# Second block's output tiles apart in PSUM, the gate as three rounded products with its embedding between tiles, the down projection's rests all on VectorE

## What is computed

```python
# first block
x = x + rms_norm(mix, g_post_mix)                        # stick-breaking and latent attention
h = rms_norm(x, g_pre_ffn)
u = causal_depthwise_conv(h @ w_up, conv_w, conv_b)
gate, val = jnp.split(u, 2, axis=-1)
f = (jax.nn.gelu(gate, approximate=True) * val) @ w_down # the down projection, 2816 -> 1024
x = x + rms_norm(f, g_post_ffn)
e = p @ w_ple                                            # the embedding, 256 -> 1024
g = jax.nn.sigmoid(rms_norm(x, g_ple_gate) @ w_ple_gate + b_ple_gate)   # the gate, 1024 -> 1024
x = x + rms_norm(g * e, g_post_ple)
# second block, all its norms scaled and shifted by mod = silu(c) @ mod_w + mod_b
mix = jnp.concatenate([y_conv, y_att, y_pool], axis=-1) @ w_out         # 1024 -> 1024
x = x + g1 * mix
h = _rmsnorm(x, norm2_g) * (1 + sc2) + sh2
x = x + g2 * _hier_moe(h, ...)     # 32 experts of width 512; each token takes 2 of one group of 8
return _rmsnorm(x, final_g)
```

## Time and profile before

| | us |
|---|---|
| median of 3 runs | 1012.39 (1012.35 to 1013.99) |
| the profiled execution, its own time | 1006.37 |
| its span | 1004.7 |
| TensorE busy | 818.2 (81%) |
| VectorE, ScalarE, POOL busy | 320.2, 300.8, 134.6 |
| share of TensorE in the chain that ended last | 53% |
| share of transfers in it | 33% |

### The profile page before, as it was taken

The page is one execution under the profiler, slowest core; times in us unless marked ns, Lnnn a source line. Parts: engine busy times, 40 slices in busy tenths (PEclk is TensorE's granted clock), DMA queues, the critical chain, the costliest instruction groups (busy, mean ns, idle before and its releaser), DMA issues.

```text
span 1004.7 us, 12218 instructions
## 1 busy us (share of the span) xinstructions
PE 818.2 (81%) x5112; PEld 518.7 (52%) x5112; DVE 320.2 (32%) x682; ACT 300.8 (30%) x606; POOL 134.6 (13%) x146
## 2 busy tenths in 40 slices
PE   6998879999998999999978899676667665566755
PEld 5856346999997874487866634312222121122213
DVE  3306555666775441349651311001000000100001
ACT  2316355666664543545442211000100000000002
POOL 0011013344443100026400000000000000000000
PEclk9999989999999999999999999879988798897879
DMA  9932964445543555562717599999999999999995
GB/s 357 428 104 87 401 256 168 167 169 187 200 159 136 189 185 234 199 242 84 264 72 317 205 423 405 430 427 428 426 428 428 427 427 429 431 427 427 427 427 234
DMA packets 23678, 297.94 MB, mean 297 GB/s; under 512 B 2752, under 2 KB 3008, under 8 KB 5440
## 3 DMA queue, kind: packets, MB, share of 16 engines
q1 hardware_dynamic: 23616, 297.09, 73.0%
HBM read 296.03 MB, written 1.05 MB: 296 GB/s over the span
## 4 chain that ended last, share of the span: by engine, by line
PE 53%; DMA 33%; DVE 6%; ACT 5%; POOL 2%; issue 1%; SPq 0%; DVEq 0%; POOLq 0%
PE ps L186 53%; DMA ring<-in_exps 32%; ACT ar L200 1%; POOL ar L217 1%; DVE ar L206 1%; ACT yT L200 1%; DVE fr L206 1%; ACT ar L197 1%; DMA ring<-in_win 1%; ACT fr L197 0%; ACT sq L200 0%; DVE yT L214 0%; DVE misc L596 0%; DVE yT L206 0%; PE ps L619 0%
## 5 line engine op out<-in xcount | busy, mean ns | idle before, releaser
L186 PE MATMUL ps<-ring,sq 128*32 128x512 f32 x976 | 146.4, 739 | 72.6 <-DMA ring<-in_exps 72.1
L186 PE MATMUL ps<-ring,ar 128*32 128x512 f32 (+3 forms) x792 | 103.9, 612 | 48.0 <-DMA ring<-in_exps 40.8
L186 PE MATMUL ps<-fr 128*128 128x256 f32 (+1 forms) x756 | 122.5, 316 | 4.7 <-DVE fr L206 4.2
L186 PEld LDWEIGHTS ps<-ring,sq 128*32 128x32 f32 x976 | 30.6, 123 | 176.9 <-DMA ring<-in_exps 119.4
L186 PEld LDWEIGHTS ps<-fr 128*128 128x128 f32 x756 | 107.1, 191 | 15.7 <-DVE fr L206 3.8
L186 PE MATMUL ps<-hT,ring 128*128 128x256 f32 (+2 forms) x416 | 93.7, 386 | 7.1 <-DMA ring<-in_win 7.1
L186 PEld LDWEIGHTS ps<-hT,ring 128*128 128x128 f32 (+2 forms) x416 | 78.3, 190 | 21.1 <-DMA ring<-in_win 7.0
L206 DVE TENSOR_TENSOR ar<-ar,ps 128x512 f32<-128x512 f32 x9 | 6.2, 686 | 257.5 <-PE ps L186 257.5
L186 PEld LDWEIGHTS ps<-ring,ar 128*32 128x32 f32 (+1 forms) x792 | 27.2, 118 | 108.8 <-DMA ring<-in_exps 63.5
L186 PE MATMUL ps<-ar 128*128 128x512 f32 (+9 forms) x320 | 65.4, 435 | 16.3 <-DVE ar L206 8.9
L206 DVE TENSOR_TENSOR fr<-ring,fr 128x512 fp32r<-128x512 f32 x75 | 62.8, 855 | 44.3 <-ACT fr L197 44.0
(11 more groups left out here) (193 smaller groups left out, 944.8 us busy)
## 6 DMA issues: line engine op xcount, KB each, us to landing
ring<-in_exps SPq DMA_DIRECT2D x90, 2048.0 KB, 30.8
ring<-in_modw SPq DMA_DIRECT2D x12, 2048.0 KB, 8.3
ring<-in_wup SPq DMA_DIRECT2D x11, 2048.0 KB, 9.0
ring<-in_win SPq DMA_DIRECT2D x5, 2048.0 KB, 11.2
ring<-in_wdown SPq DMA_DIRECT2D x5, 2048.0 KB, 8.0
ar<-in_exps SPq DMA_DIRECT2D x3, 2048.0 KB, 12.8
ring<-in_wo SPq DMA_DIRECT2D x2, 2048.0 KB, 10.1
ring<-in_wgate SPq DMA_DIRECT2D x2, 2048.0 KB, 8.6
```

The costliest lines, as they stand in the source:

```text
L186: return pe(lambda e: e.matmul(o, l, r, start=start, stop=stop, skip_group_check=True), *waits, inc=inc)
```

## The change

It has five parts.

1. *Down projection.* All rests are made by VectorE; every fourth f had one on POOL. The pieces of the last two f for n=1 are made ahead of the matmuls and squares for n=0.
2. *Gate.* Its two operands are split, and 32 fp32 products become 96 rounded ones (`gate_parts`, `gate_low`, `gate`). The rests of the weights go to POOL, but for four that go to VectorE; the rests of the activations go to VectorE, each behind the addition of the next tile; the embedding's other three quarters stand between the tiles. Both gate slots are loaded ahead of a slot of `modw` and are given free when they are split.
3. *Output tiles of the second block.* `place` puts tiles 4 to 7 in banks 6, 2, 7 and 3, each alone; tiles 0 to 3 stay in pairs in banks 4 and 5, but both of a pair are computed before either is read. Logits and sums of tiles 2 and 3 come behind tiles 4 and 5.
4. *`over_tokens`* is split in four: two parts stand behind `token_major`, two before expert slots 2 and 3; it stood behind group 1. The third pair of `first_gather` uses bank 1 for both its tiles, and the second pair uses banks 2 and 3.
5. *Slot 6* of the experts no longer waits for the router (its biases moved to `cols`), and is issued ahead of slots 10 and 11.

```diff
         def down_parts(f, n):
-            return weight_parts(w_d[f // 4].ap((f % 4) * 1024 + 512 * n, 512), p_tt if f % 4 == 3 and n else v_tt, w_d[f // 4].ready)
+            return weight_parts(w_d[f // 4].ap((f % 4) * 1024 + 512 * n, 512), v_tt, w_d[f // 4].ready)
...
+        wps = [[down_parts(f, n) for f in (20, 21)] for n in range(2)]
         for n in range(2):
-            wps = [down_parts(f, n) for f in (20, 21)]
             for j in range(2):
-                for f, (i, wh, wl, t_w) in zip((20, 21), wps):
+                for f, (i, wh, wl, t_w) in zip((20, 21), wps[n]):
...
+        GX, GW = (4096, 6144), [8192 + 1024 * k for k in range(6)] + [WP, WP + 1024]
+        w_g = [stream("wgate", n) for n in range(2)]
+        g_free, wg = {}, {}
+
+        def gate_parts(n, k):
+            h, l = fr[:, GW[k]:GW[k] + 512], fr[:, GW[k] + 512:GW[k] + 1024]
+            wg[n, k] = h, l, split(w_g[n].ap(512 * k, 512), h, l, p_tt if n == 0 or k % 2 else v_tt, w_g[n].ready, t_down, g_free.get(k))
+
...
-        t_x = add_turned(TB, lambda k: col("g_post_ffn", k), tt)
-        th = [a_fn(tile(hT, k), tile(xT, k), ACT.Copy, t_x[k], t_down, scale=col("g_ple_gate", k)) for k in range(8)]
-        embed(1, 0)
-        embed(0, 1)
-        w_p.free(embed(1, 1))
+        for k in range(4):
+            gate_parts(0, k)
+        t_x, th = [], []
+
+        def gate_low(k):
+            hi, lo = (tile(fr, k, o) for o in GX)
+            t = a_fn(hi, tile(xT, k), ACT.Copy, t_x[k], t_down, scale=col("g_ple_gate", k))
+            th.append(v_stt(lo, tile(xT, k), col("g_ple_gate", k), hi.bitcast(F32), ALU.mult, ALU.subtract, t))
+
+        for k in range(8):
...
+            if k:
+                gate_low(k - 1)
+            if k == 3:
+                embed(1, 0)
+            elif k == 5:
+                embed(0, 1)
+            elif k == 7:
+                w_p.free(embed(1, 1))
+        gate_low(7)
+        for k in range(4, 8):
+            gate_parts(0, k)
+        w_g[0].free([wg[0, k][2] for k in range(4, 8)])
...
+        def gate(j, n, k):
...
+            mm(o, xh, wh, k == 0, False, t_w, th[k], read[ZB[j, n]])
+            mm(o, xl, wh, False, False)
+            t_gz[j, n] = g_free[k] = mm(o, xh, wl, False, k == 7, inc=1)
...
             for j in range(2):
-                o = k * S + 128 * j
-                t_gz[j, 0] = mm(bank(ZB[j, 0]), hT[:, o:o + 128], w.ap(k * 512, 512), k == 0, k == 7, w.ready, th[k],
-                               read[ZB[j, 0]], inc=int(k == 7))
+                gate(j, 0, k)
+            gate_parts(1, k)
...
-        rbias = ar[:, rbo:rbo + 36]
+        rbias = col("router_b", 0, 36)
...
+        place = {k: (4 + k // 2, S * (k % 2)) for k in range(4)}
+        place.update({4: (6, 0), 5: (2, 0), 6: (7, 0), 7: (3, 0)})
...
+        for i in range(2):
+            t = [wout2_tile(2 * i + n, (2, 3, 4, 5)) for n in range(2)]
+            for n in range(2):
+                residual(2 * i + n, t[1])
...
+        for k in range(4, 8):
+            t = wout2_tile(k, (0, 1, 6, 7, 2, 3, 4, 5))
+            if k < 6:
+                tile_logits(k - 2)
+                tile_squares(k - 2)
+            residual(k, t)
+            if k == 6:
+                for p in (4, 5):
+                    tile_logits(p)
+                    tile_squares(p)
...
+        def over_tokens(i):
+            for c in range(4):
+                k = 4 * (i % 2) + c
+                mm(bank(YB[i], 128 * c, 128 * c + 128), xT[:, k * S + 128 * (i // 2):k * S + 128 * (i // 2) + 128], ident,
+                   c == 0, False, tt[k], read[YB[i]])
+
+        for i in (2, 3):
+            over_tokens(i)
...
-        more = {3: ("more3", [hT[:, :], ar[:, 1536:3584]], t_early), 6: ("more6", spare, [t_arena, t_lg, read[LG]])}
+        more = {3: ("more3", [hT[:, :], ar[:, 1536:3584]], t_early), 6: ("more6", spare, t_arena)}
...
-                b, c = 2 + 2 * (p % 3) + k % 2, 0
+                b, c = (1, 128 * (k % 2)) if p == 2 else (2 + k % 2, 0)
...
-        placed = {j: stream("exps", j, extra=more.get(j)) for j in (0, 1, 2, 4, 3, 5, 7, 8, 9, 10, 11, 6)}
+        placed = {j: stream("exps", j, extra=more.get(j)) for j in (0, 1, 2, 4, 3, 5, 7, 8, 9, 6, 10, 11)}
...
+                    if j in (2, 3):
+                        over_tokens(j - 2)
...
-            if g == 1:
-                over_tokens()
```

More of the change, by code:

```diff
@@ L969, in build @@
                 r3, t_r3 = row_root(3, 32 * 1024, 120, t, S)
-        w.free(t_gz[1, 0])
-        w = stream("wgate", 1)
+        w_g[1].free([wg[1, k][2] for k in range(8)])
         for j in range(2):
             for k in range(8):
-                o = k * S + 128 * j
-                t = mm(bank(ZB[j, 1]), hT[:, o:o + 128], w.ap(k * 512, 512), k == 0, k == 7, w.ready, read[ZB[j, 1]], inc=int(k == 7))
-            t_gz[j, 1] = t
-        w.free(t)
+                gate(j, 1, k)
         for n in range(2):
@@ L1305, in wout2_tile @@
         def wout2_tile(k, ks):
-            i, n = k // 2, k % 2
-            b = 4 + i
+            b, o = place[k]
             for kk_ in ks:
-                t = mm(bank(b, n * S, n * S + S), w_2[i // 2].ap(kk_ * 512 + 256 * (i % 2) + 128 * n, 128), tile(yT, kk_),
-                       b not in started, kk_ == ks[-1], w_2[i // 2].ready, mixed[kk_], read[b], inc=int(kk_ == ks[-1]))
+                t = mm(bank(b, o, o + S), w_2[k // 4].ap(kk_ * 512 + 256 * (k // 2 % 2) + 128 * (k % 2), 128), tile(yT, kk_),
+                       b not in started, kk_ == ks[-1], w_2[k // 4].ready, mixed[kk_], read[b], inc=int(kk_ == ks[-1]))
@@ L1311, in wout2_tile, with residual @@
                 started.add(b)
+            return t
+        def residual(k, t):
+            b, o = place[k]
             x = tile(xT, k)
-            tt.append(v_stt(x, bank(b, n * S, n * S + S), mod[:, 16 + k:17 + k], x, ALU.mult, ALU.add, t, t_mod))
-            read[b] = tt[-1]
-            t_sq[k] = a_fn(tile(sq, k), x, ACT.Square, tt[-1], t_rc)
-            return t
-        for k in range(8):
-            t = wout2_tile(k, (2, 3, 4, 5) if k < 4 else (0, 1, 6, 7, 2, 3, 4, 5))
-            if k == 3 or k == 7:
-                w_2[k // 4].free(t)
-            for p in {3: (0, 1), 5: (2, 3), 6: (4, 5)}.get(k, ()):
-                tile_logits(p)
-                tile_squares(p)
+            read[b] = t = v_stt(x, bank(b, o, o + S), mod[:, 16 + k:17 + k], x, ALU.mult, ALU.add, t, t_mod)
+            tt.append(t)
+            t_sq[k] = a_fn(tile(sq, k % 4), x, ACT.Square, t, t_rc, t_sums.get(k - 4))
@@ new lines, in build @@
+        for i in range(2):
+            t = [wout2_tile(2 * i + n, (2, 3, 4, 5)) for n in range(2)]
+            for n in range(2):
+                residual(2 * i + n, t[1])
+            if i:
+                w_2[0].free(t[1])
+            if i:
+                for p in range(2):
+                    tile_logits(p)
[8 more added lines that the diff above has]
+                for p in (4, 5):
+                    tile_logits(p)
+                    tile_squares(p)
@@ L1325, in build @@
+        w_2[1].free(t)
         tile_logits(6)
```

31 lines of the change are left out of this document (18 added, 13 removed).

## The result

| | before | after |
|---|---|---|
| median of 4 runs, us | 1012.37 (1011.33 to 1013.99) | 995.85 (994.03 to 998.01) |
| the profiled execution, its own time | 1006.37 | 995.91 |
| its span | 1004.7 | 994.1 |

The ratio is 0.985, with an interval from 0.9818 to 0.9882. The forecast for the traced execution was 995.5 us and a span of 993.8; it came out at 995.91 and 994.1. (How far single executions of the kernel before differ, and what of the 16.5 us is chance, is the subject of the first experiment.)

A forecast was written before the change was run, and what follows sets the result against it. The end was taken to follow TensorE's use of slot 12; gains of 1.3 + 4.0 + 5.9 + 2.4 = 13.6 less 2.7 gave 10.9 us, so 995.5 for the traced execution and 1001.5 against the median, range 997.5 to 1005.5.

The forecast's parts named there:

- slot 0 at full clock: Rival, chance 0.15: expert slot 0 runs at 2.4 GHz and takes 1.7 us less; 12.6 in all, 999.8.
- Third f: Down projection: the last rest, moved from POOL to VectorE, is done 1.2 to 1.8 us earlier; 1.3 taken.
- Last two f: Down projection: pieces made ahead remove 2.27 us of idle time and 1.74 of half clock, 4.0 us.
- Gate: Gate product: 96 rounded products at 21.8 us replace fp32 ones at 27.8; gain 5.9 us after the switch.
- Tiles: Second block's output tiles: three odd tiles no longer wait for VectorE's read, 0.8 us each, 2.4 gained.
- x products: Token sums (over_tokens): eight products between slots 1 and 3 lose 1.9 us; eight before the rank's matmul are hidden.
- gathers: First gather, third pair: sharing bank 1, the second half waits for VectorE's read; 0.8 us lost, lower bound 0.5.
- Between 12 and 19: Expert slots: TensorE's way from slot 12's issue to slot 19's grows by 2.7 us, from 35.6 to 38.3.
- the end hangs on slot 19: Expert stream: slot 19 waits for TensorE's use of slot 12; behind it 77 slots at 4.91 us set the end.
- POOL did not starve the gate: Rival, chance 0.04: POOL's rests come too late for the gate's matmuls, making the kernel slower, 1014.4 and up.
- The stream followed: Rival, expert stream does not follow: 998.8 if the 2.7 us are all hidden, 1012.4 if something else holds it.
- Lost cover: Rival, chance 0.13: a late square, rest or clock fall in a denser stretch gives back 2 to 7 us, 1003.5 to 1008.5.

The follow-up runs named there:

- the first experiment: The kernel before, run again without an edit: ratio 1.0004 (0.9972 to 1.0035), 12 executions from 1005.76 to 1015.65 us.
- x_late: The changed kernel with the eight x products that stood before expert slots 2 and 3 put behind group 1: 994.43 us, ratio 0.9853.
- x_late_banks: The changed kernel with those eight x products behind group 1 and the third gather pair in banks 4 and 5: 994.94 us, ratio 0.9849.
- after_again: The changed kernel run once more, without a further edit: 996.09 us, ratio 0.9875, 6 executions from 995.07 to 999.63 us.
- best: x_late_banks plus 13 products of constants, which nobody reads, in TensorE's idle stretches at 73 to 77 us and 175 us: 991.30 us, ratio 0.9802.
- down_only: The kernel before with only the down projection's edits (all rests on VectorE, last two f's pieces made ahead): 1004.63 us, ratio 0.9948.

## Why the prediction was too careful

**The step that failed** is the last of the sum: "The median of the runs shown is 1012.39, 6.0 above the profiled one, so I set the difference against it: 1001.5." The sum itself was made for the traced execution, and there it gives 995.5 where 995.91 was measured. That it comes so close is in part luck: slot 19 went out at 597.93, 1.5 us earlier than the 599.4 forecast, and the stream behind it took 1.9 us longer than before in this one execution. I then carried the 6.0 us over as if they were a fixed addition that the changed kernel pays too. They were not: they are the distance between a lower and an upper execution of a kernel whose times have two heaps. The heaps' means are 7.1 us apart. After, there are no such heaps in 10 executions, and trace and median agree (995.91 and 995.85). Half of the executions of before lie in the upper heap; that all four first runs did was chance.

Against the mean of 108 executions the forecast difference of 10.9 would have given 999.8, inside the range and still 3.3 above the mean of after, 996.5. The rival below, with its 12.6, gives 998.1. The 1.6 us that are then left are over twice the standard error of the mean gain with all chips pooled (0.65), but on the one chip on which both kernels ran side by side nothing is left: the gain there is 12.5.

**The rival that came true**, in part beside the forecast: *slot 0 at full clock*. I gave it 0.15 because the matmuls ahead of slot 0 stay thin. Slot 0 is at full clock in both traces of the changed kernel; in the first it brought 1.56 us of the 1.7 forecast. With it the sum for slot 19 is 12.6; 12.37 was measured.

**The terms.** Third f 1.1 for 1.3: VectorE's rest begins when its own queue allows it, and TensorE is still idle for 1.30 us. Last two f 4.0 for 4.0. Gate 5.64 for 5.9. Tiles 2.5 for 2.4. x products -2.1 for -1.9, by a single edit; gathers -0.8 for -0.8, by an edit that also gives ScalarE its part back. Between 12 and 19 2.89 for 2.7. No term is off by more than 0.3 us.

**The structure.** That the end hangs on slot 19 held in the changed kernel: three kernels that issue it at different times (596.08 `x_late`, 600.83 `x_late_banks`, 597.93 after) end 378 to 380 us later. No matmul of the gate waits for a transfer.

**The other rivals.** POOL did not starve the gate: no row of it waits for POOL. The stream followed. *Lost cover* by a new fall of the clock happens in the changed kernel too: `after_again` has the clock at 0.75 over 76.6 to 83.4 us, the first trace of after at 0.50 from 495.0 to 505.2. The latter gave nothing back: the matmuls ahead of it and behind it lie 11.38 us earlier than before alike (487.97 against 499.35, 501.33 against 512.71). These rows answer to that:

```profile
76.60:83.40 6.80, 6.16 (x38) 4.80 (x39) 5.12 (x6) 5.39 (x8) 0.00 (x0) 0.75 0.60 255
```

```profile
495.00:505.20 10.20, 7.09 (x24) 5.02 (x26) 5.43 (x16) 3.42 (x13) 0.00 (x0) 0.50 0.04 18
```

**What is shown and what is not.** Shown: that executions of before lie up to 12 us apart (1004.9 to 1016.7); that falls of the clock that cost 1.6 to 3.1 us each come and go in code that is the same; that a kernel with products in two idle stretches (`best`) has a mean about 3 us below that of the kernel without them, across two chips. Argued only: that the upper heap of before is made of such falls alone, since no upper execution of before itself was traced, and that the fillers work by keeping the clock up. With products in three idle stretches of the kernel before (`fillers`) the spread was narrower, but the gain in the mean is not clear of noise. Open: whether tracing itself keeps an execution out of the upper heap; why `down_only` narrows the spread (a standard deviation of 1.5 us) when neither of its edits does so as well alone; whether anything stands behind the distance of the mean gain, 14.2 us or 12.5 by one chip, to the 12.4 that the traced pair shows at slot 19; and why eight products ahead of the rank keep slot 0's clock up in the changed kernel and not in the kernel before. (The Trainium skill, TensorE: Matmul & The Clock Gate, Part 1, says that the chip's own count of activity runs freely beside the kernel, so that the point at which the clock changes varies between runs. The traces agree that it varies; they do not show that count.)

## What to carry to other kernels

Before a difference worked out from one trace is set against a median, place the traced execution among many executions of the same kernel: here they lay in two heaps 7 us apart, and the first runs all fell into the upper one. Where the clock falls behind a short idle stretch of TensorE, the stretch costs twice, the idle time and here up to 3.1 us of half speed, and not in every execution. Cheap products put into such stretches are worth a try, with ten or more executions of each kernel on the same chip as the measure and not one trace: here one such try was clear of noise and one was not. A saving counts where its stage's last wait is: here ahead of slot 12, while the eight x products placed between slots 1 and 3, behind the issue of slot 12, were paid in full.

## What the runs showed of the hardware

- The same 32 records of TensorE took 3.18 us in one execution and 5.72 in another (granted clock 1.00 and 0.50), with no edit ahead of them.
- Such falls came behind idle stretches as short as 1.29 and 0.96 us with a few matmuls between, and at one of 1.57 us. The same stretches were followed by a clock of 1.00 in the first trace of before.
- A rounded product of 512 columns took 0.230 us in the gate (72 from 388.26 to 404.80), an fp32 one two records of 0.433 each (48 from 395.39 to 416.17); three rounded products for one fp32 product saved 20% of its time.
